# Second block, attention turns: other places for the shares, transposes, strips and memory steps, and a fourth low part on VectorE

## The reference, cut to what matters

```
h = rms_norm_2(x, g_pre)
proj = h @ w_in
(a_val, a_gate, sq, sk, sv, s_gate, ..., mq, m_gate, g_logits) = split(proj)
y_a = pool_mixer(a_val, a_gate, w_pool, scale)
y_b = swa_mixer(sq, sk, sv, s_gate)
y_c = gla_mixer(...)
y_m = mem_attn(mq, m_gate, mem, g_mem, w_mem_kv)
```

## Time and profile before, and how to read it

| | us |
|---|---|
| median of 3 runs | 3214.67 |
| lowest and highest run | 3212.93, 3218.14 |
| the profiled execution | 3221.14 |
| its span, first to last instruction | 3219.1 |
| TensorE busy | 3135.8 (97%) |
| VectorE busy | 1780.5 (55%) |
| ScalarE busy | 1422.6 (44%) |
| GpSimd busy | 1099.8 (34%) |
| mean granted clock of TensorE | 0.989 |

### The profile page before, as it was taken

The page is one execution under the profiler, slowest core; times in us unless marked ns, Lnnn a source line. Parts: engine busy times, 40 slices in busy tenths (PEclk is TensorE's granted clock), DMA queues, the critical chain, the costliest instruction groups (busy, mean ns, idle before and its releaser), DMA issues.

```text
span 3219.1 us, 43126 instructions
## 1 busy us (share of the span) xinstructions
PE 3135.8 (97%) x15938; PEld 2650.3 (82%) x15938; DVE 1780.5 (55%) x2330; ACT 1422.6 (44%) x2180; POOL 1099.8 (34%) x460
## 2 busy tenths in 40 slices
PE   9999999999999999999999999878999999999999
PEld 8877788888888888877888888767788888888887
DVE  3573321012123544377787776786118999999802
ACT  6543322333236534334545555433435555555532
POOL 7633323434442434353544444344330000000043
PEclk9999999999999999999999999989999999999999
DMA  8632322333433423343333333333654444444442
GB/s 290 177 92 66 86 72 79 87 83 99 122 113 93 138 71 89 92 124 92 101 94 101 89 105 95 108 92 104 209 158 134 131 136 139 139 134 137 139 155 98
DMA packets 551652, 375.30 MB, mean 117 GB/s; under 512 B 19288, under 2 KB 505688, under 8 KB 550232
## 3 DMA queue, kind: packets, MB, share of 16 engines
q1 hardware_dynamic: 526448, 327.79, 35.4%
q10 hardware_dynamic: 25064, 45.60, 4.0%
HBM read 338.73 MB, written 34.60 MB: 116 GB/s over the span
## 4 chain that ended last, share of the span: by engine, by line
PE 84%; DVE 10%; POOL 2%; issue 2%; ACT 1%; DMA 1%; DVEq 0%; ACTq 0%; SPq 0%; POOLq 0%
PE proj L937 35%; PE t L1559 13%; PE s L1559 10%; PE proj L1559 7%; PE s L1829 3%; POOL w_lo L905 2%; DVE w_lo L3734 2%; PE proj L1829 1%; PE s L1407 1%; PE t L1829 1%; DVE p_s L4022 1%; PE t L962 1%; PE s L962 1%; PE s L1006 1%; PE s L999 1%
## 5 line engine op out<-in xcount | busy, mean ns | idle before, releaser
L894 POOL TENSOR_TENSOR w_lo<-raw,w_hi 128x1024 fp32r<-128x1024 f32 x303 | 758.1, 2513 | 1660.4 <-ACT w_hi L1866 1622.0
L937 PE MATMUL proj<-ht_hi,w_hi 128*128 128x512 f32 x1376 | 549.2, 399 | 0.0
L937 PE MATMUL proj<-ht_hi,w_lo 128*128 128x512 f32 x1376 | 536.6, 390 | 0.0
L937 PE MATMUL proj<-ht_lo,w_hi 128*128 128x512 f32 x1376 | 535.9, 389 | 0.0
L1866 ACT ACTIVATE w_hi<-raw 128x1024 fp32r<-128x1024 f32 x264 | 272.3, 1054 | 404.8 <-PE proj L937 234.7
L905 POOL TENSOR_TENSOR w_lo<-raw,w_hi 128x1024 fp32r<-128x1024 f32 x96 | 262.4, 2748 | 411.7 <-ACT w_hi L2550 411.7
L937 PEld LDWEIGHTS proj<-ht_lo,w_hi 128*128 128x128 f32 x1376 | 258.6, 188 | 56.0 <-issue 3.8
L937 PEld LDWEIGHTS proj<-ht_hi,w_hi 128*128 128x128 f32 x1376 | 258.5, 188 | 55.4 <-issue 3.8
L937 PEld LDWEIGHTS proj<-ht_hi,w_lo 128*128 128x128 f32 x1376 | 258.3, 188 | 54.7
L2550 ACT ACTIVATE w_hi<-t_w 128x1024 fp32r<-128x1024 f32 x96 | 101.6, 1059 | 174.8 <-DVE t_w L3741 90.2
L4119 DVE TENSOR_TENSOR w_lo<-raw,w_hi 128x1024 fp32r<-128x1024 f32 x128 | 156.2, 1220 | 15.4 <-ACT w_hi L2848 14.4
(11 more groups left out here) (750 smaller groups left out, 6774.1 us busy)
## 6 DMA issues: line engine op xcount, KB each, us to landing
raw<-in_w_in_dram SPq DMA_DIRECT2D x404, 512.0 KB, 3.8
raw<-in_w_out_dram SPq DMA_DIRECT2D x64, 512.0 KB, 4.0
g_zt<-z_spill SPq DMA_DIRECT2D x64, 256.0 KB, 3.8
z_spill<-z_late ACTq DMA_DIRECT2D x36, 256.0 KB, 2.4
raw<-in_xa_wkv_dram SPq DMA_DIRECT2D x16, 512.0 KB, 7.4
raw<-in_w_mem_kv_dram SPq DMA_DIRECT2D x16, 512.0 KB, 3.6
raw<-in_w_br_gla_dram SPq DMA_DIRECT2D x16, 512.0 KB, 3.9
raw<-in_w_br_pool_dram SPq DMA_DIRECT2D x16, 512.0 KB, 4.3
```

What stands on the lines that cost most here:

```text
L894: pool.tensor_tensor(w_lo[:, slot, :], raw[:, slot, :], w_hi[:, slot, :].bitcast(F32), ALU.subtract).then_inc(lo_done, 1)
L937: ins = pe.matmul(dst, w, x[:, kt, c0:c1], start=first and n == 0 and m == 0, stop=last and n == len(kts) - 1 and m == 2)
```

## The change

It moves steps in the hand-written orders of TensorE, ScalarE and VectorE, and gives the low part `lt3` of product 4 from GpSimd to VectorE, behind the "window" work and ahead of `v`. VectorE gets a new place "late", behind `f22`. No arithmetic changes. The head that was collected in turns 5, 10 and 15 has its shares late in that turn and all transposes and values in the next; the last head (turns 20 and 21) keeps its order but for two ScalarE steps. The local logits go from the third turn's window to its late place. The strips are divided: four operations stay in turn 0, 18 go to turn 1's window. The memory steps on TensorE stand one half product later, and `mem_y` goes from the middle to the late place.

```diff
-        swa_act = events("swa_act", "e2 z w n0 n1 c0 n2 n3 c1 c2 c3")
+        swa_act = events("swa_act", "e2 z w n0 n1 c0 c1 n2 n3 c2 c3")
...
-        duo_dve = Order(sem("duo_dve"), "lt2 t3 f21 t4 v c12 f12 t1 lb11 c22 f22 lt1 t2 c11 f11", "t1 lb11 lt1 t2", "f21")
+        duo_dve = Order(sem("duo_dve"), "lt2 t3 f21 t4 lt3 v c12 f12 t1 lb11 c22 f22 lt1 t2 c11 f11", "t1 lb11 lt1 t2", "f21")
...
-        duo_pool = Order(sem("duo_pool"), "lb22 lt3 lb21 lt4")
+        duo_pool = Order(sem("duo_pool"), "lb22 lb21 lt4")
...
                 duo_low(t, 3, "hb22", right(t)[1], "lb22")
-                duo_low(t, 4, "ht3", right(t)[0], "lt3")
                 duo_low(t, 5, "hb21", B21, "lb21")
...
+                if i < SWA_HPG - 1:
+                    return {8: lambda: swa_natural(i)}
...
+                if i < SWA_HPG - 1:
+                    def opened():
+                        swa_back(i)
+                        swa_probs(i, 0)
+
+                    return {1: opened, 2: lambda: swa_probs(i, 1), 4: lambda: swa_values(i, 0), 5: lambda: swa_values(i, 1),
+                            10: lambda: swa_probs(i, 2), 11: lambda: swa_probs(i, 3), 13: lambda: swa_values(i, 2),
+                            14: lambda: swa_values(i, 3), **other}
...
-                duo_pair(t + 2, {1: lambda: swa_scores(i, 0), 3: lambda: swa_vt(i, 1)})
+                duo_pair(t + 2, {4: lambda: swa_scores(i, 0), 6: lambda: swa_vt(i, 1)})
...
-                last = {5: lambda: mem_probs(i - 1, (0, 1)), 7: lambda: mem_probs(i - 1, (2, 3)),
-                        9: lambda: mem_values(i - 1)} if i else {}
-                return last if i == MEM_HEADS else {**last, 11: lambda: mem_scores(i)}
+                last = {6: lambda: mem_probs(i - 1, (0, 1)), 8: lambda: mem_probs(i - 1, (2, 3)),
+                        10: lambda: mem_values(i - 1)} if i else {}
+                return last if i == MEM_HEADS else {**last, 12: lambda: mem_scores(i)}
...
-                return {0: lambda: swa_exps(i, 2), 1: lambda: swa_gate(i), 2: lambda: swa_rates(i), 3: lambda: swa_near(i),
-                        5: lambda: both(lambda: swa_copy(i, 0), lambda: swa_far(i)), 6: lambda: swa_copy(i, 1)}
...
+                first = {0: lambda: swa_exps(i, 2), 1: lambda: swa_gate(i)}
+                if i < SWA_HPG - 1:
+                    return {**first, 5: lambda: both(lambda: swa_rates(i), lambda: swa_near(i))}
+                return {**first, 2: lambda: swa_rates(i), 3: lambda: swa_near(i), 5: lambda: swa_copy(i, 0),
+                        6: lambda: both(lambda: swa_copy(i, 1), lambda: swa_far(i))}
...
+                return {1: lambda: both(lambda: swa_copy(i, 0), lambda: swa_copy(i, 1)),
+                        3: lambda: both(lambda: swa_far(i, (1,)), lambda: swa_vt(i + 1, 0)), 4: lambda: swa_far(i, (2,)),
+                        5: lambda: both(lambda: swa_copy(i, 2), lambda: swa_copy(i, 3))}
...
-                    0: lambda: mem_exps(n), 1: lambda: mem_weighted(n), 2: lambda: mem_copies(n, (0, 1)),
-                    3: lambda: mem_copies(n, (2, 3)), 5: lambda: y_store(SWA_HPG + n, c_z[n % 2][:]), **gate}
...
+                    0: lambda: mem_exps(n), 1: lambda: mem_weighted(n), 3: lambda: mem_copies(n, (0, 1)),
+                    4: lambda: mem_copies(n, (2, 3)), 5: lambda: y_store(SWA_HPG + n, c_z[n % 2][:]), **gate}
...
                 then("window")
+                duo_low(t, 4, "ht3", right(t)[0], "lt3")
                 after(dve, "sv", t)
...
+                then("late")
                 if t < DUOS - 1:
                     duo_second(t + 1)
...
+            def far_strips():
+
                 ROUND = 1.5 * 2.0 ** 23
...
+                if i < SWA_HPG - 1:
+                    return {"window": opened, "late": lambda: swa_shares(i)}
                 return {"window": window, "middle": lambda: swa_classes(i)}
...
-                         {"window": lambda: swa_y(i - 1)} if i else {})
+                         {"window": (lambda: swa_classes(i - 1)) if i else far_strips})
...
-                         {"window": lambda: swa_logits(i, 0)})
+                         {"late": lambda: swa_logits(i, 0), **({"front": lambda: swa_y(i - 1)} if i else {})})
...
-                          "middle": lambda: mem_y(i - 2), "end": lambda: mem_logits(i - 1)})
+                          "late": lambda: mem_y(i - 2), "end": lambda: mem_logits(i - 1)})
```

More of the change, by code:

```diff
@@ L1625, in swa_vt @@
                 if g == 0 and i:
-                    wait(pe, swa_act, "c3", i - 1)
-                elif g:
+                    wait(pe, swa_act, "c0", i - 1)
+                elif g == 1 and i:
+                    wait(pe, swa_act, "c2", i - 1)
+                if g:
                     pe.wait_ge(att_vc, i * 3 + MO_HEADS + g)
@@ L1645, in swa_probs @@
                     wait(pe, swa_act, f"c{x - 2}", i)
-                elif x == 0:
+                if x == 0:
                     pe.wait_ge(att_vc, i * 3 + MO_HEADS + 3)
+                elif x == 2 and i < SWA_HPG - 1:
+                    pe.wait_ge(att_vc, i * 3 + MO_HEADS + 4)
                 c0, c1 = SWA_SETS[x]
@@ L2669, in swa_near, with swa_far @@
                         ins.then_inc(swa_act.sem, 1)
-            def swa_far(i):
+            def swa_far(i, gs=(1, 2)):
                 wait(act, swa_dve, "back", i)
-                for g in range(1, 3):
+                for g in gs:
                     for b in range(NT):
@@ L3939, in swa_first, with opened, window @@
             def swa_first(i):
-                def window():
+                def opened():
                     swa_spread(i)
                     swa_gate(i)
+                def window():
+                    opened()
                     swa_shares(i)
+                if i < SWA_HPG - 1:
+                    return {"window": opened, "late": lambda: swa_shares(i)}
                 return {"window": window, "middle": lambda: swa_classes(i)}
@@ L4096, in _ @@
                 if g == 0:
-                    first = {"front": lambda: mem_gate(n), "window": opened, "middle": lambda: mem_y(n - 1),
+                    first = {"front": lambda: mem_gate(n), "window": opened, "late": lambda: mem_y(n - 1),
                              "end": lambda: mem_logits(n)}
-                    second = {"window": first_sums, "middle": lambda: mem_y(n), "end": lambda: pool_lows(0)}
+                    second = {"window": first_sums, "late": lambda: mem_y(n), "end": lambda: pool_lows(0)}
                 else:
```

18 lines of the change are left out of this document (9 added, 9 removed).

## The result

The changed kernel takes 3196.43 us (median of 4 runs, 3195.12 to 3199.97) where the kernel before, run beside it, takes 3215.08: a ratio of 0.9942, 95% interval 0.993 to 0.9954, so 18.7 us faster.

The account below looks back on a forecast made before the run. It took TensorE to bound the kernel, with waits set by VectorE, which GpSimd stretches, and partly a lower clock. Terms 0 - 4.9 + 3.2 - 8.5 - 3.8 = -14.0 us took 3214.7 to 3200.7 us; range 3181 to 3211.

Parts of the forecast that it names:

- the logits: Third turns of four heads: late local logits delay the next turn, product 4 waits 1.2 us for v; 6.0 us lost.
- Strips: Turns 0 and 1: 8.2 us gained in turn 0, 8.4 lost in turn 1; taken as 0, ends -6.5 and +1.
- Heads 0 to 2: Attention turns: moved shares end waits (-12.4), second-turn waits +1.5, late local logits +6.0; -4.9 us, ends -10.9 and +4.
- Last head: Turns 20 and 21: a longer wait for v (+1.1) and a held low part (+2.1); +3.2 us, ends -2 and +5.
- the two short waits become one of about 3.2 us: Turn 20: v comes behind the low part, giving one longer TensorE wait with slow matmuls; +1.1 us.
- Memory steps: Turns 22 to 24: later TensorE requests end the waits for probabilities and slow halves; -8.5 us, ends -10.5 and -4.
- Pool turns: Turns 25 on: fewer GpSimd holds bring v slightly earlier, turn 25 gains 1.2, the next 1.0; -3.8 us, ends -8 and 0.
- the prediction's own sign: Pool turns: the prediction calls itself wrong if they change by more than 2 us each.
- VectorE's queue becomes the bound: Rival, chance 0.05: product 4's low part is held behind window work in ten turns; kernel slower, +18, 3233 us.
- the lucky case: Rival, chance 0.28: moved work finds cover everywhere, logits and turn 21 cost nothing, strips one hold less; -26, 3188 us.
- The rival in which the waits move and stay: Rival, chance 0.12: memory waits turn up again at product 3, 8.5 shrinks to 2; 3207 to 3212 us.
- second price: TensorE: after a wait of 2 us or more the next matmuls run slower; 2.8 us more after turn 15's wait.

Follow-up runs that it names:

- run 3: Changed kernel with the second group's scores one product later on TensorE in turns 3, 8, 13 and 18: 3190.02 us, ratio 0.9922.
- run 4: Changed kernel with the local logits back in the third turn's window, ahead of product 4's low part and v: 3185.77 us, ratio 0.9908.
- run 2: Kernel before with only product 4's low part moved from GpSimd to VectorE: 3212.83 us, ratio 0.9986.
- run 6: Changed kernel with the memory attention's output on VectorE back in the middle place, ahead of t1: 3209.72 us, ratio 0.9976.
- run 7: Changed kernel with TensorE's four memory steps back at their old places, half a product earlier: 3210.12 us, ratio 0.9981.
- run 8: Kernel before with only the memory attention's output on VectorE moved late, behind f22: 3217.51 us, ratio 1.0005.
- run 1: Changed kernel with product 4's low part given back to GpSimd, the moved order kept: 3208.46 us, ratio 0.998.

## Why the prediction was right, step by step

The sum was -14.0 us; the median moved by 18.7. On the two traces, of which the first is the one that the sum was made on, the span moved by 21.0, the stretch of the turns by 22.4 and turn 31's wait for v by 1.3 more (10.13 to 8.87). Turn 0 began 1.0 us later, and the rest lies outside the turns, where executions differ: turn 0 begins anywhere from 1453.9 to 1459.0 us in the runs above, which are the same up to there. The terms were not all right, and two errors of opposite sign went together: the logits cost 5.5 us more than forecast, the pool turns gave 7.4 more. That the time came out as near as it did is in part luck.

- **Strips**, forecast 0: turn 0 is 8.4 us shorter, turn 1 7.3 longer, so -1.1. The wait in turn 1 was 5.28 for 6.3, with two holds, as worked out.
- **Heads 0 to 2**, forecast -4.9: -1.4. The shares' move gave 19.0 in the turns 5, 10 and 15 and took 5.5 in 6, 11 and 16, all of it work that came over: -13.5, where -10.9 stood (-12.4, and 1.5 for waits in the second turns that didn't come). No run moves the shares alone; that their waits are gone is read from the rows. The step that failed is the logits, 4 times 1.5: it is 4 times 2.9, 11.5 us, and at another place. I let the 3.2 us run on to v ("product 4, due at +12.0, waits 1.2"); they met the key sum first, which the scores need in the middle of product 1, with slow products behind the wait in turn 18 (runs 3 and 4). The remaining 0.7 is spread over the other eight turns.
- **Last head**, forecast +3.2: +0.1. In turn 21 the +2.1 came as +1.95. In turn 20 the step "the two short waits become one of about 3.2 us" was wrong: the wait was 1.85, and the turn gained 1.8. The sum freed one hold; in the rows both the spread and the gate are free (0.22 and 0.68 us, 2.38 and 2.88 before), and v came 1.8 us earlier in the turn. And 1.6 of the gain hang on the clock, which fell behind this same wait in runs 2 and 4, whose turn 20 takes 25.1 and 25.0 us, and not in the other nine traces that have it (rows at the end).
- **Memory steps**, forecast -8.5: -10.1 in the turns 22 to 24. The size was near: the waits that went are 5.3 us and the slower matmuls 4.8 (TensorE busy 76.29 and 71.49 us, at a granted clock of 0.96 and 1.00). The reason was half of it. The later transposes were needed, but so was the output's place on VectorE, which the prediction counted only ahead of t1 in the turns 25 and 26 (runs 6 to 8). The short waits for ScalarE's copy that I expected in their place didn't come, and that is the whole difference.
- **Pool turns**, forecast -3.8 with ends -8 and 0: -11.2, beyond its end. Turns 25 and 26 gave 7.0 where I had 2.2: the order alone gave 4.5 there, the low part alone 3.4 (runs 1 and 2), and with the output back in the middle they take 55.4 us, more than before (run 6). Of the 7.0, waits are 3.8 and shorter matmuls 3.2 (turn 25 ran at a granted clock of 0.89 before and runs at 1.00 now); the sum has no term for slow matmuls in these turns. By the prediction's own sign, no pool turn changing by more than 2 us, this term was wrong: turn 25 fell by 5.4, turn 27 by 2.1. VectorE's timeline of turn 25 before, from the first of the window's held operations to v:

```profile
2042.89 2.62 DVE L4022 TENSOR_TENSOR p_s<-p_u 128x512 f32<-128x512 f32 x1
...
2046.27 2.25 DVE L4027 TENSOR_TENSOR p_p<-p_s,p_rc 128x16 f32<-128x16 f32 x1
2048.56 2.28 DVE L4028 TENSOR_TENSOR p_p<-p_p,p_u 128x16 f32<-128x16 f32 x1
...
2052.64 0.42 DVE L3755 TENSOR_TENSOR d_v<-proj,d_v 128x256 f32<-128x256 f32 x1
```

  And now, with GpSimd's two low parts beside it:

```profile
2032.66 2.28 DVE L4057 TENSOR_TENSOR p_p<-p_s,p_rc 128x16 f32<-128x16 f32 x1
2034.98 2.29 DVE L4058 TENSOR_TENSOR p_p<-p_p,p_u 128x16 f32<-128x16 f32 x1
2037.19 1.21 DVE L3754 TENSOR_TENSOR w_lo<-raw,w_hi 128x1024 fp32r<-128x1024 f32 x1
2038.32 0.41 DVE L3775 TENSOR_TENSOR d_v<-proj,d_v 128x256 f32<-128x256 f32 x1
```

```profile
2032.51 2.40 POOL L905 TENSOR_TENSOR w_lo<-raw,w_hi 128x1024 fp32r<-128x1024 f32 x1 [4.42 <-ACT w_hi L2564]
2034.86 2.37 POOL L905 TENSOR_TENSOR w_lo<-t_w,w_hi 128x1024 fp32r<-128x1024 f32 x1
```

  GpSimd holds two operations of the window, where it held three before; v ends 14.65 us into the turn (first matmul at 2024.08), before at 17.5 (first matmul at 2035.57).

The rival on the other side (VectorE's queue becomes the bound) fell: product 4 waits for v behind window work in seven turns, but by more than 0.2 us longer than before in two only (1 and 21). The result lies between the forecast and the lucky case (3188), nearer to the forecast, but not by that rival's reasons: the logits did cost, the strips had both holds, and turn 21 lost its 1.95. What was beyond the forecast came mostly from the pool turns and turn 20, which it doesn't name. The rival in which the waits move and stay has its case in the strips and in the new wait for the key sum, but not in the memory steps, on which its price hangs.

The Trainium skill ("Perfetto Trace Analysis", section "Optimizing Scalar/DVE Operations") says that moving work between GpSimd and VectorE might not help. The runs show that here it did, by an amount that depends on the order around it: alone the move gave 4.5 us, in the new order 12. The Trainium skill's page "SBUF — State Buffer", section "SBUF: two separate sides", says that the port pair which the two share is an exclusive lock for a whole instruction. The rows agree: in turn 25 GpSimd's low parts end at 2034.91 and 2037.23 us and the two held operations at 2034.94 and 2037.27, and one of 16 columns takes 2.28 us where it takes 0.17 a little earlier in the same turn.

## What to carry to other kernels

Two engines that lock each other out are to be placed by where their long operations fall, not by their sums: one low part less on GpSimd was worth 12 us in one order and 4.5 in the other. When a block moves behind other work, list every result that now comes later and ask where its first reader stands; here it was the scores of the next turn, and not v. Where an output frees a bank, the place that writes it and the place that wants the bank move together or not at all: here the one without the other gave nothing (runs 6 and 8).

## Not expected of the hardware

A wait's second price varies from one execution to the next. With the same wait of 6.08 to 6.10 us in turn 27, product 4 then took 4.19 us in the changed kernel, 4.36 with the output in the middle, 4.98 with the low part alone and 5.22 with the early memory steps, where 2.77 is usual. Product 4 of turn 20, in the changed kernel and in run 4:

```profile
1915.79 2.05 PE L1558 MATMUL proj<-ht_lo,w_hi 128*128 128x512 f32 x8 [1.85 <-DVE d_v L3775]
...
1917.82 1.19 PE L1558 MATMUL proj<-ht_lo,w_lo 128*128 128x256 f32 x8
```

```profile
1901.39 2.82 PE L1558 MATMUL proj<-ht_lo,w_hi 128*128 128x512 f32 x8 [1.86 <-DVE d_v L3775]
...
1904.30 1.90 PE L1558 MATMUL proj<-ht_lo,w_lo 128*128 128x256 f32 x8
```

The turn runs at a mean granted clock of 1.00 in the first and of 0.93 in the second, and takes 23.42 and 25.02 us. The turns 8 and 18 of the changed kernel have waits of 2.18 and 2.19 us and take 23.27 and 24.77. So turns with equal waits differ by up to 1.6 us here, and a sum over turns is no finer than this. The prediction charged the second price to waits of 2 us or more. The rows don't show such a line: turn 25 now runs at 1.00 with a wait of 2.63 us, and the slow half in the earlier trace rows stood behind one of 1.92 (turn 23 before).
